# One 512-wide matmul for high weights times high and low activations in the 256-token output and down projections

## The reference, cut to what matters

```python
return jnp.matmul(o.astype(h.dtype), w_out)        # hybrid mixer: w_out, 1024 x 1024
return jnp.matmul(o, wo)                           # cross-attention: wo, 1024 x 1024
return jnp.matmul(jax.nn.silu(gate) * val, w_down) # feed-forward: 2816 x 1024
out_x = blocked_attention(q_x, k_all, v_all) @ w_o[j]   # second block: wo2, 1024 x 1024
x = x + mx[5] * out_x
```

## Time and profile before

| | |
|---|---|
| median of 3 runs | 2330.72 us (2329.1 to 2333.82) |
| profiled execution, its own time | 2335.02 us |
| its span | 2333.2 us |
| TensorE (PE) busy | 2163.9 us, 93% |
| VectorE (DVE) busy | 1013.3 us, 43% |
| ScalarE (ACT) busy | 788.7 us, 34% |
| mean granted TensorE clock | 0.956 |
| DMA mean | 135 GB/s |

### The profile page before, as it was taken

How to read it: one execution, slowest core, us unless ns; L and a number is a source line. 1 busy time by engine, 2 the same in 40 slices (tenths; PEclk the granted TensorE clock), 3 DMA queues, 4 the chain that set the end, 5 groups by cost and what they waited for, 6 DMA issues and landing times.

```text
span 2333.2 us, 31359 instructions
## 1 busy us (share of the span) xinstructions
PE 2163.9 (93%) x13698; PEld 1832.7 (79%) x13698; DVE 1013.3 (43%) x1286; ACT 788.7 (34%) x968; POOL 239.7 (10%) x207
## 2 busy tenths in 40 slices
PE   7977789899989999999899999999999998988998
PEld 6856479799958888877767888876887886848997
DVE  4565665575762232234444233225222223745454
ACT  4531144454543222224223222224221222444443
POOL 0200300031301101110010100110100111001101
PEclk9977689999989999999999999999999999999999
DMA  6550444345472232234233222244224223353453
GB/s 246 201 205 20 173 147 171 144 146 189 169 265 99 72 117 94 70 129 148 76 136 139 79 104 108 71 147 180 86 86 181 82 75 119 109 201 143 165 192 105
DMA packets 53544, 314.23 MB, mean 135 GB/s; under 512 B 5920, under 2 KB 11936, under 8 KB 23584
## 3 DMA queue, kind: packets, MB, share of 16 engines
q1 hardware_dynamic: 51216, 309.48, 37.2%
q10 hardware_dynamic: 2192, 2.75, 0.4%
HBM read 311.16 MB, written 1.05 MB: 134 GB/s over the span
## 4 chain that ended last, share of the span: by engine, by line
PE 85%; DVE 7%; ACT 3%; DMA 2%; issue 2%; POOL 0%; SPq 0%; ACTq 0%; DVEq 0%; POOLq 0%
PE psum L236 26%; PE psum L238 25%; PE psum L237 25%; DMA raw<-in_mod 2%; PE psum L1413 2%; ACT w_hi L212 1%; DVE w_lo L220 1%; PE psum L1146 1%; PE psum L1124 1%; PE psum L326 1%; DVE work L373 0%; PE psum L1138 0%; DVE xc L1266 0%; PE psum L1514 0%; DMA raw<-in_w_in_a 0%
## 5 line engine op out<-in xcount | busy, mean ns | idle before, releaser
L236 PE MATMUL psum<-xn_hi,w_hi 128*128 128x256 f32 (+1 forms) x2504 | 846.8, 338 | 35.3 <-DVE xn_lo L366 16.2
L237 PE MATMUL psum<-xn_lo,w_hi 128*128 128x256 f32 (+1 forms) x2504 | 841.6, 336 | 0.0
L238 PE MATMUL psum<-xn_hi,w_lo 128*128 128x256 f32 (+1 forms) x2504 | 841.1, 336 | 0.0
L220 DVE TENSOR_TENSOR w_lo<-raw,w_hi 128x2048 fp32r<-128x2048 f32 (+1 forms) x246 | 508.3, 2067 | 483.6 <-ACT w_hi L212 483.3
L236 PEld LDWEIGHTS psum<-xn_hi,w_hi 128*128 128x128 f32 x2504 | 483.1, 193 | 93.0 <-issue 42.7
L237 PEld LDWEIGHTS psum<-xn_lo,w_hi 128*128 128x128 f32 x2504 | 483.4, 193 | 47.0 <-issue 0.5
L238 PEld LDWEIGHTS psum<-xn_hi,w_lo 128*128 128x128 f32 x2504 | 482.5, 193 | 46.9
L212 ACT ACTIVATE w_hi<-raw 128x2048 fp32r<-128x2048 f32 (+1 forms) x246 | 421.7, 1714 | 195.4 <-PE psum L238 170.0
L236 PE MATMUL psum<-h_hi,w_hi 128*128 128x512 f32 (+1 forms) x880 | 307.1, 349 | 3.6 <-POOL h_lo L1388 3.6
L237 PE MATMUL psum<-h_lo,w_hi 128*128 128x512 f32 (+1 forms) x880 | 306.7, 348 | 0.0
L238 PE MATMUL psum<-h_hi,w_lo 128*128 128x512 f32 (+1 forms) x880 | 306.6, 348 | 0.0
(11 more groups left out here) (331 smaller groups left out, 1420.0 us busy)
## 6 DMA issues: line engine op xcount, KB each, us to landing
raw<-in_mod SPq DMA_DIRECT2D x72, 1024.0 KB, 4.8
raw<-in_a_up SPq DMA_DIRECT2D x42, 1024.0 KB, 4.8
raw<-in_b_up SPq DMA_DIRECT2D x42, 1024.0 KB, 4.8
raw<-in_ffn_up SPq DMA_DIRECT2D x22, 1024.0 KB, 4.9
raw<-in_a_down SPq DMA_DIRECT2D x32, 704.0 KB, 4.0
raw<-in_b_down SPq DMA_DIRECT2D x32, 704.0 KB, 4.1
raw<-in_ffn_down SPq DMA_DIRECT2D x16, 704.0 KB, 4.1
raw<-in_w_in_a SPq DMA_DIRECT2D x8, 1024.0 KB, 5.8
```

What stands on the lines that cost most here:

```text
L220: dve.tensor_tensor(w_lo[:, slot, 0:size], raw[:, raw_slot(("main", g)), 0:size], w_hi[:, slot, 0:size].bitcast(F32), ALU.subtract).then_i ...
L236: pe.matmul(out, lh, rh, start=first, stop=False, skip_group_check=group)
L237: pe.matmul(out, lh, rl, start=False, stop=False, skip_group_check=group)
L238: return pe.matmul(out, ll, rh, start=False, stop=last, skip_group_check=group)
```

## The change

The high and low activations become one tile each, `xn` and `h`, with an axis of two for high and low, in the places where the two tiles lay. A new helper `pe_both_halves` issues, for each input and output tile, one matmul of the high weights with 512 columns, namely the 256 tokens of the high part and then the 256 of the low part, into a whole bank, and a second one of the low weights with the 256 columns of the high part into the first half of the bank. VectorE then adds both halves of the bank into `xc` (`dve_add_both`): all first halves of the chunk, a wait for a semaphore of its own, all second halves. It is used for `w_out`, `wo`, `wo2` and the down projections of `ffn` and `b2`; the 512-token layers stay as they are.

```diff
-        xn_hi = sb("xn_hi", [P, KT, 2 * T], F32R)
-        xn_lo = sb("xn_lo", [P, KT, 2 * T], F32R)
+        xn = sb("xn", [P, 2, KT, 2 * T], F32R)
+        xn_hi, xn_lo = xn[:, 0, :, :], xn[:, 1, :, :]
...
+        def pe_both_halves(pe, job, act, n_tiles=2, k_tiles=KT, before_k=None):
+            for s in steps(job):
+                bank_free(pe, s)
+                pe.wait_ge(lo_ready, s.g + 1)
+                for k in range(k_tiles):
+                    if before_k is not None:
+                        before_k(s, k)
+                    for n in range(n_tiles):
+                        w = slice((n * k_tiles + k) * P, (n * k_tiles + k + 1) * P)
+                        pe.matmul(psum[:, s.bank + n, :], w_hi[:, s.slot, w], act[:, :, k, X], start=(k == 0), stop=False)
+                        mm = pe.matmul(psum[:, s.bank + n, X], w_lo[:, s.slot, w], act[:, 0, k, X], start=False, stop=(k == k_tiles - 1))
+                mm.then_inc(chunk_done, 1)
...
+        def dve_add_both(dve, tiles, gate):
+            def evac(s):
+                dve.wait_ge(chunk_done, s.g + 1)
+                for half in (X, C):
+                    for n in range(tiles):
+                        k = s.c * tiles + n
+                        x, got = xc[:, k, X], psum[:, s.bank + n, half]
+                        if gate is None:
+                            mm = dve.tensor_tensor(x, x, got, ALU.add)
+                        else:
+                            mm = dve.scalar_tensor_tensor(x, got, gate[:, k, 0:1], x, ALU.mult, ALU.add)
+                    if half is X:
+                        halves_count[0] += 1
+                        mm.then_inc(halves_added, 1)
+                        dve.wait_ge(halves_added, halves_count[0])
+                mm.then_inc(evacuated, 1)
+            return evac
...
-        h_hi = sb("h_hi", [P, HALF, 2 * T], F32R, scope=later)
-        h_lo = sb("h_lo", [P, HALF, 2 * T], F32R, scope=later)
+        h = sb("h", [P, 2, HALF, 2 * T], F32R, scope=later)
+        h_hi, h_lo = h[:, 0, :, :], h[:, 1, :, :]
...
-            pe_feature_major(pe, jobs["wo"], xn_hi, xn_lo, X)
+            pe_both_halves(pe, jobs["wo"], xn)
...
-            run_dve(dve, jobs["wo"], dve_add_gated(dve, 2, None, 1))
+            run_dve(dve, jobs["wo"], dve_add_both(dve, 2, None))
```

More of the change, by code:

```diff
@@ L1268, in dve_add_gated @@
             return evac
+        halves_added = sem("first_half_added")
+        halves_count = [0]
+        def dve_add_both(dve, tiles, gate):
[15 more added lines that the diff above has]
+            return evac
         ff_gate, ff_hi, ff_lo, ff_conv, ff_tap = (sem(x) for x in (
@@ L1307, in hidden_k @@
                             pe.wait_ge(ff_lo, base + (HALF - 1 if k == 0 else HALF))
-                    pe_feature_major(pe, down, h_hi, h_lo, slice(0, self.w), n_tiles=1, k_tiles=HALF, before_k=hidden_k)
+                    if self.w == T:
+                        pe_both_halves(pe, down, h, n_tiles=1, k_tiles=HALF, before_k=hidden_k)
+                    else:
+                        pe_feature_major(pe, down, h_hi, h_lo, slice(0, self.w), n_tiles=1, k_tiles=HALF, before_k=hidden_k)
             def act(self, act, then):
@@ L1375, in dve @@
                         late()
-                    run_dve(dve, jobs[f"{self.name}_down{half}"], dve_add_gated(dve, 1, self.gate, self.w // T))
+                    run_dve(dve, jobs[f"{self.name}_down{half}"],
+                            dve_add_both(dve, 1, self.gate) if self.w == T else dve_add_gated(dve, 1, self.gate, self.w // T))
             def pool(self, pool):
@@ L1676, in mixed_k @@
                     pe.wait_ge(post_lo, k // 2 + 1)
-            pe_feature_major(pe, jobs["w_out"], xn_hi, xn_lo, X, before_k=mixed_k)
+            pe_both_halves(pe, jobs["w_out"], xn, before_k=mixed_k)
             mod_turn(pe)
@@ L1752, in _ @@
             pe.wait_ge(at_lo, att1.heads + att2.heads)
-            pe_feature_major(pe, jobs["wo2"], xn_hi, xn_lo, X)
+            pe_both_halves(pe, jobs["wo2"], xn)
             n25.pe(pe)
@@ L1860, in _ @@
             mod_rows_out(dve)
-            run_dve(dve, jobs["w_out"], dve_add_gated(dve, 2, None, 1))
+            run_dve(dve, jobs["w_out"], dve_add_both(dve, 2, None))
             mod_columns(dve)
@@ L1937, in _ @@
             mod_columns(dve)
-            run_dve(dve, jobs["wo2"], dve_add_gated(dve, 2, gate_of(4), 1))
+            run_dve(dve, jobs["wo2"], dve_add_both(dve, 2, gate_of(4)))
             n25.dve(dve)
```

## The result

| | median | runs |
|---|---|---|
| changed kernel | 2341.43 us (2338.29 to 2343.86) | 6 |
| before, on the same chip | 2329.82 us (2324.26 to 2333.82) | 6 |

The ratio of the changed kernel's time to the time before is 1.005 (95% interval 1.0035 to 1.0066), or 11.6 us more (8 to 15). The forecast was 2340.9 us in a range of 2335.5 to 2346.5, slower by 10.2 us; the measured time lies in that range, 0.5 us from it.

What follows compares the result with a forecast made beforehand. The prediction took TensorE to be bound by matmul columns plus 7 to 13 ns a matmul, with almost no slack in the ring in `wo`. Its terms summed to +10.2 us on the median of 2330.72: 2340.9 us, range 2335.5 to 2346.5.

Steps and rivals of the forecast that it cites:

- `wo`, ring to the last square: In `wo`, second adds lengthen the turn from 5.46 to 6.24 us, over TensorE's 5.55: +2.03 us until the norm's last square.
- `wo`, clock behind it: Behind `wo`, TensorE stands nearly idle and the granted clock falls, slowing the next job's matmuls: +1.0 us (0 to 3).
- `ffn_down0`: In `ffn_down0`, 88 pairs each cost 6.7 ns more and the extra add fits in VectorE's wait: +0.59 us.
- `ffn_down1`, ring: In `ffn_down1`, seven turns each 0.44 us longer: +3.08 us to the split, +3.52 to the last square, taken as +3.3.
- `wo2`, ring to the last square: In `wo2`, the turn grows from 5.59 to 6.50 us against a period of 5.76: +2.93 us before the norm of `b2`.
- `wo2`, clock behind it: Behind `wo2`, the fall of the granted clock is there already, so no added cost.
- `b2_down0`: In `b2_down0`, 88 pairs each cost 6.7 ns more and the extra add fits in VectorE's wait: +0.59 us.
- `b2_down1`: In `b2_down1`, last chunk ends 0.1 us sooner, last second half adds 0.51, little or no wait: +0.39 us (0.3 to 1.0).
- The ring: Add, square, `w_hi`, `w_lo`, next add in `wo`, `wo2`, `ffn_down1`: almost no slack in `wo`, so second adds lengthen each turn.
- The rival of hidden adds: Turns have slack of 0.8 us, so TensorE's pace rules everywhere and second adds are hidden: +2.1 us, 2332.8; 12%.
- The pair's price: A 512-wide plus a 256-wide matmul in changed jobs takes 346.7 ns, against 360 for three with `xn`, 340 with `h`.
- The clock: Granted clock falls when TensorE idles: +1.0 us (0 to 3) behind `wo`; behind `wo2` and `ffn_down1` the fall is there already.

Runs made afterwards that it cites:

- e2: Kernel before with its three 256-wide matmuls, but every tile of the changed jobs added twice, with the semaphore between: 2341.58 us, ratio 1.0052.
- e3: Whole changed kernel, with each chunk's square moved behind the next chunk's `w_hi` in ScalarE's queue: 2332.14 us, ratio 0.9999 to before.
- e5: Changed kernel, 512-wide matmuls reading adjoining columns of `xn` in `wo`, `wo2`, `ffn` down jobs, two pieces of `xn` in `b2` down jobs: 2341.82 us, one run.
- e1: Changed kernel with the adds of the second halves taken out, so the sum lacks high weights times low activations: 2331.49 us, ratio 1.000.
- e6: Change kept in `ffn_down0` and `b2_down0` alone, the rest as in the kernel before: 2329.23 us, ratio 0.9988.
- e7: Changed kernel with idle 512-wide matmuls behind `wo` (14) and `wo2` (14, and 8 ahead of `b2_up0`): 2339.69 us, ratio 1.0035 to before.
- e10: Whole changed kernel with late squares and all the idle matmuls of e9: 2326.81 us, ratio 0.9985 to before.
- e9: e8 with four more idle 512-wide matmuls ahead of the wait for the last `h_lo` in each `ffn` down job: 2324.89 us, ratio 0.9975.
- e8: e4 with 8 idle 512-wide matmuls ahead of each of `w_in_a`, `w_out`, `ab_a`, `k2` and `b2_up0`: 2324.62 us, ratio 0.9964.
- e4: Kernel before with each chunk's square moved behind the next chunk's `w_hi` and nothing else: 2326.88 us, ratio 0.9988.

## Why the prediction was right

By its steps, in us:

| step | forecast | measured |
|---|---|---|
| `w_out`, pairs at 346.7 ns | -0.64 | 347 ns, -0.63 in the last three chunks; whole stretch -1.2 |
| `wo`, ring to the last square | +2.03 | +2.14 |
| `wo`, clock behind it | +1.0 | +0.43 |
| `ffn_down0` | +0.59 | -0.61 |
| `ffn_down1`, ring | +3.3 (3.52 to the square) | +3.63 to the square; about +3.8 at `a1_up0` |
| `wo2`, ring to the last square | +2.93 | +2.94 |
| `wo2`, clock behind it | 0 | +0.95 |
| `b2_down0` | +0.59 | +1.15 |
| `b2_down1` | +0.39 | +0.60 |
| sum | +10.2 | +10.2; medians +11.6 (8 to 15) |

The 0.5 us by which the first chunk of `w_out` is shorter can't be put down to the change: that chunk has two lengths, in kernels of both forms.

**The ring** was the mechanism and carries nearly all of it. Its turns came out at 6.25 (forecast 6.24) in `wo`, 6.49 (6.50) in `wo2`, 4.17 (4.15) in `ffn_down1`. e2 shows that the adds make it, e3 that they do so through the square in ScalarE's queue. The rival of hidden adds fell for the reason given: 0.2 us of slack against 0.78 needed. In e3, where `wo` has 1.4 us of slack, the time is that of before, as that rival has it.

**`ffn_down1` to `a1_up0`** is the changed stretch on which a single pair of profiles would have misled: 63.96 against 62.51. It moves by some 2 us from kernel to kernel, and why is open. The kernels with the slow ring have 63.96, 64.77 (e5), 64.41 and 66.32, a mean of 64.9; those with the ring of before (before, e1 and e6) have 62.51, 60.07 and 60.78, a mean of 61.1. That is the +3.8 of the table, a difference of averages over few kernels. The five with late squares have 57.36 to 61.85, a mean of 59.9, with an earlier last square; the term is good to a microsecond at best.

**The pair's price** was up to 7 ns too low. With `xn` it is 347 (`w_out`, `wo2`) or 353 ns (`wo`) for the 346.7 forecast. With `h` it is 353: the sum of two rows of 512-wide and 256-wide matmuls with `h` (233.3 + 113.3) missed by 6.7 ns, since the 256-wide one takes 118 here and the 512-wide one 235. This is the mis-sized term behind `b2_down0` (+1.15 for +0.59) and behind the 0.2 us missing in `b2_down1`, whose last chunk starts its last matmul 0.1 us later and not sooner. By the Trainium skill, "TensorE: Matmul & The Clock Gate", section "Back-to-back issue gap", an estimate for a pair from the gap that it gives for isolated matmuls is 325.0 ns. The trace doesn't agree: no chunk of pairs in any run here averages under 346 ns.

**The clock** is the step that failed, in both places. I gave it 1.0 us behind `wo`, where it cost 0.43, and nothing behind `wo2`, "the fall is there already". It was there, but began only behind the norm's last four matmuls (granted 1.00 up to 2130, these end at 2129.9). In the changed kernel these four come 2.9 us later against the job's start, the fall (granted 0.51 from 2129 to 2130) begins ahead of them and nearly doubles them, +0.95. e7 takes both away and gets back 0.41 and 0.92. The two errors cancel to 0.4 us, and those of the two `down0` to 0.6 the other way: that the sum comes so near is in part luck.

**`ffn_down0`** had the wrong sign. Its edit costs 1.0 us (e10 against e9); that it looks like a gain comes from a fall of the clock in the kernel before (e9 without it: 1.6 us less), which I didn't look for.

What stays open: why `ffn_down1`, with the same 1.81 us of waiting for `h_lo`, keeps a granted clock of 1.00 behind it in the kernel before while `ffn_down0` doesn't; and 1.4 us between the sum of the steps and the medians, inside the interval.

## What to carry to other kernels

Merging matmuls could save only what each costs beyond its columns, 7 to 13 ns here; with `xn` it saved 7 to 13 ns a group, with `h` it saved nothing and cost 13 where groups of three stood 340 ns apart. Where the results must be added by another engine, the adds are to be priced in that engine's place in the order of work and not by its busy share: VectorE was 43% busy, and 0.8 us more of adds a chunk still made the four chunks of `wo` 2.1 us longer. Before such a change look for an operation that waits in an in-order queue ahead of work that others need; moving the square one chunk back took the changed kernel from a ratio of 1.005 to 0.9999, and the old kernel with late squares and idle matmuls beats both (e8, 0.9964, 0.995 to 0.9978), though no run shows which of the two does it. And compare stretches over several kernels: the two profiles alone said 3.9 us for an effect of 11.6.

## What the runs showed that I had not expected

- The same code has two spacings. In `b2_down1`, groups of three passes stand 353 ns apart before and in e6, 340 in e4; `w_out`'s pairs 347 in the changed kernel and 353 in e5. Within a kernel the spacing changes from chunk to chunk (e6: the first chunk of `b2_down1` 340, the others 353). What decides it stays open. TensorE in `b2_down1`, before and then in e4, ten groups each:

```profile
2315.00 0.28 PE L236 MATMUL psum<-h_hi,w_hi 128*128 128x256 f32 x1
...
2318.53 0.28 PE L236 MATMUL psum<-h_hi,w_hi 128*128 128x256 f32 x1
```

```profile
2306.17 0.28 PE L236 MATMUL psum<-h_hi,w_hi 128*128 128x256 f32 x1
...
2309.57 0.28 PE L236 MATMUL psum<-h_hi,w_hi 128*128 128x256 f32 x1
```

- A moving operand of 512 columns in two pieces 4096 columns apart costs what one piece costs (350 ns a pair in e5).
- In `ffn_down0` an idle time of 1.80 to 1.81 us was followed by a second chunk at half the granted clock (5.36 us) in all four kernels that have it, and one of 1.69 to 1.73 us by a second chunk of 3.9 us in the six where I read it.
